# One decoder layer on one core: the input normalised in three token groups ahead of the memory tokens

## The reference

```python
n1 = rms_norm(x, g_mix)                        # x * rsqrt(mean(x*x) + 1e-6) * g_mix
qa, ka, va, qr, kr, vr, gr = split(n1 @ w_in)  # 512, 128, 128, 256, 256, 512, 512 columns
att = window_attention(qa, ka, va, sinks)      # window 128, with ALiBi
ret = retention(qr, kr, vr)
h = x + merge(att, groupnorm(ret) * silu(gr)) @ w_out
mn = rms_norm(mem_prompt, g_mem)               # 256 memory tokens
mk, mv = mn @ w_xk, mn @ w_xv                  # needed by the cross attention, and outputs p_mem_k, p_mem_v
h = h + cross_attend(rms_norm(h, g_xattn), mk, mv)
h = h + square(relu(rms_norm(h, g_mlp) @ w_up)) @ w_down
y = rms_norm(h, g_final)
```

## Time and profile before

| what | value |
|---|---|
| median of three runs | 1641.11 us |
| the profiled execution | 1644.39 us, of it the span 1642.6 us |
| PE busy in the span | 1536.9 us (94%) |
| DVE, ACT, POOL busy | 645.1, 442.3, 246.3 us |
| mean granted clock of PE | 0.968 of full speed |

### The profile page before, as it was taken

The page is one execution under the profiler, slowest core; times in us unless marked ns, Lnnn a source line. Parts: engine busy times, 40 slices in busy tenths (PEclk is TensorE's granted clock), DMA queues, the critical chain, the costliest instruction groups (busy, mean ns, idle before and its releaser), DMA issues.

```text
span 1642.6 us, 25177 instructions
## 1 busy us (share of the span) xinstructions
PE 1536.9 (94%) x9990; PEld 1479.1 (90%) x9990; DVE 645.1 (39%) x1169; ACT 442.3 (27%) x791; POOL 246.3 (15%) x276
## 2 busy tenths in 40 slices
PE   5959999989699999788999999999999999999998
PEld 5959988878599999787888999999999999999997
DVE  3542466455644442243337432234322332233322
ACT  3541244333311111242214331123201330123212
POOL 2010000042236600112435000000000000000143
PEclk9979999999779999899999999999999999999999
DMA  5751110020332131022553111111111111111112
GB/s 175 211 207 44 35 39 14 14 62 13 121 114 58 41 101 39 13 103 91 167 167 103 42 48 52 38 52 41 49 51 39 51 39 52 51 40 51 39 39 106
DMA packets 152618, 115.38 MB, mean 70 GB/s; under 512 B 12880, under 2 KB 141968, under 8 KB 152272
## 3 DMA queue, kind: packets, MB, share of 16 engines
q1 hardware_dynamic: 140816, 72.49, 15.3%
q0 software_dynamic: 10576, 37.66, 6.6%
q10 hardware_dynamic: 1152, 4.19, 0.7%
HBM read 101.19 MB, written 14.16 MB: 70 GB/s over the span
## 4 chain that ended last, share of the span: by engine, by line
PE 82%; issue 7%; DVE 5%; DMA 3%; ACT 2%; POOL 1%; SPq 0%; DVEq 0%; ACTq 0%; POOLq 0%
PE ps L351 23%; PE ps L352 23%; PE ps L353 23%; PE ps L1047 4%; PE ps L1333 2%; PE ps L1351 2%; DVE wlo L340 1%; PE ps L1110 1%; PE ps L1131 1%; DMA raw<-in_w_xv 1%; ACT whi L324 1%; DVE xlo L1478 1%; DMA raw<-in_w_xk 1%; PE ps L1197 0%; DMA out_p_mem_v<-mkv 0%
## 5 line engine op out<-in xcount | busy, mean ns | idle before, releaser
L351 PE MATMUL ps<-xhi,whi 128*128 128x352 f32 x1392 | 457.7, 329 | 15.7 <-DVE wlo L340 8.3
L352 PE MATMUL ps<-xlo,whi 128*128 128x352 f32 x1392 | 450.0, 323 | 0.0
L353 PE MATMUL ps<-xhi,wlo 128*128 128x352 f32 x1392 | 449.6, 323 | 0.0
L351 PE MATMUL ps<-yhi,whi 128*128 128x352 f32 x1152 | 374.1, 325 | 5.9 <-DVE wlo L340 2.1
L352 PE MATMUL ps<-ylo,whi 128*128 128x352 f32 x1152 | 370.1, 321 | 0.0
L353 PE MATMUL ps<-yhi,wlo 128*128 128x352 f32 x1152 | 369.9, 321 | 0.0
L351 PEld LDWEIGHTS ps<-xhi,whi 128*128 128x128 f32 x1392 | 264.9, 190 | 23.6 <-issue 12.5
L352 PEld LDWEIGHTS ps<-xlo,whi 128*128 128x128 f32 x1392 | 265.0, 190 | 0.1
L353 PEld LDWEIGHTS ps<-xhi,wlo 128*128 128x128 f32 x1392 | 264.1, 190 | 0.0
L324 ACT ACTIVATE whi<-raw 128x1024 fp32r<-128x1024 f32 x126 | 132.9, 1055 | 427.9 <-PE ps L353 400.9
L351 PEld LDWEIGHTS ps<-yhi,whi 128*128 128x128 f32 x1152 | 216.9, 188 | 8.6 <-DVE wlo L340 3.9
(11 more groups left out here) (267 smaller groups left out, 1353.1 us busy)
## 6 DMA issues: line engine op xcount, KB each, us to landing
raw<-in_w_up SPq DMA_DIRECT2D x32, 512.0 KB
raw<-in_w_down SPq DMA_DIRECT2D x32, 512.0 KB
raw<-in_w_xo SPq DMA_DIRECT2D x16, 512.0 KB
kx<-in_cache_mem_k POOLq DMA_DIRECT2D x16, 512.0 KB, 5.0
raw<-in_w_in SPq DMA_DIRECT2D x14, 512.0 KB, 3.8
spill<-hT POOLq DMA_DIRECT2D x8, 528.0 KB, 6.2
hT<-spill POOLq DMA_DIRECT2D x8, 528.0 KB, 5.1
raw<-in_w_xk SPq DMA_DIRECT2D x8, 512.0 KB
```

What stands on the lines that cost most here:

```text
L351: pe.matmul(out, whi[:, q, k, :], x1, start=k == 0, stop=False)
L352: pe.matmul(out, whi[:, q, k, :], x2, start=False, stop=False)
L353: mm = pe.matmul(out, wlo[:, q, k, :], x1, start=False, stop=k == KB - 1)
```

## The change

The order of the first stages is turned round, and the x tokens are taken in three groups of 384, 384 and 288.

- **Loads.** SP issues them: identity and ones first, then the x tiles into nine buffers, with the first two units set between them, and all later units in one order. ACT issues the load of `g_mix`. POOL loads memory tokens, the rest of the tables and the other vectors later.
- **Groups.** As soon as three tiles are turned and copied, ACT and DVE make `xhi` and `xlo` of this group alone, and only then the squares, 1/rms and diagonals. 1/rms is a power -0.5 on POOL (`mean_root`); the root and reciprocal on ACT and DVE go away.
- **First two units** (keys, values): chunk by chunk over both units, as each group comes (`first_product`).
- **Memory units.** Order of units: keys, values, query unit 0, eight units of `w_xk`, query unit 1, eight units of `w_xv`, query units 2 and 3. The memory tokens are turned inside query unit 0, the memory keys turned back inside query unit 1, the memory values inside query unit 2 (16 transposes each), each stored when its copies are done.
- **Places.** `xin`, `diag`, `mnhi` and `mnlo` lie behind `za`'s sixth block, `mkvT` and `mkv` over `hT`; so DVE waits for the residual spill ahead of the memory units and for the stores of the memory keys and values ahead of unit `U_RET`, where `zb` takes the place.

The core of the diff (line numbers of the new kernel differ):

```diff
+FIRST = ["k", "v", 0] + ["mk"] * 8 + [1] + ["mv"] * 8 + [2, 3]
+CHUNKS = [1 if f in ("mk", "mv") else NCH for f in FIRST]
+U_Q0, U_MK, U_Q1, U_MV = 2, 3, 11, 12
+U_IN = 16
...
@@ SP
+            sp.dma_start(tab[:, 0:2 * P], io["tables"][:, 0:2 * P]).then_inc(s_first, 16)
+            for t in range(3):
+                x_load(t)
+            first_unit(0)
+            x_load(3)
+            first_unit(1)
+            for t in range(4, XT):
+                x_load(t)
+            for u in range(2, U_RET):
+                first_unit(u)
@@ POOL
+            pool.wait_ge(S("dve_constants"), 3)
+            mean_root(0, 0, 3)
+            pool.wait_ge(*x_ready(5))
+            pool.dma_start(memx[:], io["mem_prompt"][0].rearrange("(t p) d -> p t d", p=P)).then_inc(s_tab, 16)
+            pool.dma_start(tab[:, 2 * P:], io["tables"][:, 2 * P:]).then_inc(s_tab, 16)
...
             for k in range(KB):
                 pool.dma_start(spill[k], hT[:, k, :]).then_inc(s_spill, 16)
+            mean_root(2, 6, XT)
+            mean_root(3, XT, XT + 2)
@@ ACT
+                act.dma_start(gains[:, G_MIX, :], io["g_mix"][0].rearrange("(k p) -> p k", p=P)).then_inc(s_first, 16)
...
+            act.wait_ge(s_first, 32)
...
+            for t in range(3):
+                x_keep(t)
+            split_hi(act, 0, 0)
+            first_hi(0)
+            x_keep(3)
+            squares_x(0)
+            split_hi(act, 1, 1)
+            x_keep(4)
+            x_keep(5)
+            rstd_x(0)
+            first_hi(1)
+            squares_x(1)
...
+            for u in range(U_MK, U_IN + 4):
+                split_hi(act, u + 1, (u + 1) % 2)
+                if u == U_Q1:
+                    kv_keep(0)
+                    kv_keep(2)
@@ PE
+            for t in range(4):
+                turn_x(t)
+            first_product(0, 0)
+            turn_x(4)
+            turn_x(5)
+            spread_rstd(0)
+            first_product(1, 0)
+            turn_x(6)
+            first_product(0, 1)
+            turn_x(7)
+            turn_x(8)
+            spread_rstd(1)
+            first_product(1, 1)
+            first_product(0, 2)
+            spread_rstd(2)
+            first_product(1, 2)
...
+            for u in range(U_MK, U_Q1):
+                pe.wait_ge(s_wlo, u + 1)
+                product(pe, u, u % 2, 0, mnhi, mnlo, NM)
+            u = U_Q1
+            pe.wait_ge(s_wlo, u + 1)
+            product(pe, u, 1, 0, xhi, xlo, CW)
+            pe.wait_ge(s_ev, chunks_before(u))
+            for s in range(4):
+                turn_kv(s)
...
@@ DVE
+            def first_evacuate(q, c):
+
+                dve.wait_ge(s_rstd, c + 1)
+                dve.wait_ge(s_mm, 2 * c + q + 1)
+                dve.tensor_tensor(za[:, 4 + q, c * CW:(c + 1) * CW], ps[:, q, 0:CW], rstd[:, c * CW:(c + 1) * CW], ALU.mult).then_inc(s_ev, 1)
...
-            dve.wait_ge(s_mout, 48)
-            run(U_IN, 2, scaled(za, U_IN - 4))
-            run(U_IN + 2, 2, scaled(za, U_IN + 2))
...
+            dve.wait_ge(s_spill, 16 * KB)
+            for u in range(U_MK, U_IN + 4):
+                split_lo(dve, u + 1, (u + 1) % 2)
...
-            dve.wait_ge(s_spill, 16 * KB)
+            dve.wait_ge(s_mout, 48)
             for n in range(NQ):
```

More of the change, by code:

```diff
@@ L120, in tables, with chunks_before @@
     return t.astype(np.float32), s.astype(np.float32)
-def chunks_before(u, memory=False):
-    if memory or (isinstance(u, int) and u <= U_IN):
-        return u
+def chunks_before(u):
+    if isinstance(u, int) and u < U_RET:
+        return sum(CHUNKS[:max(u, 0)])
     return u * 3 - 2 * U_IN
@@ new lines, in x_keep, with first_hi @@
+            def x_keep(t):
+                w = P if t < NQ else TS
+                act.wait_ge(s_xT, t + 1)
+                copy(hT[:, 0:4, t * P:t * P + w], ps[:, 2 + 2 * (t % 2), :].rearrange("p (k t) -> p k t", k=4)[:, :, 0:w]).then_inc(s_xea, 1)
+            def first_hi(g):
+                for k in range(KB):
+                    act.wait_ge(s_xea if k < 4 else s_xed, min(3 * g + 3, XT))
+                    act.activation(xhi[:, k, group(g)], hT[:, k, group(g)], ACT.Copy, scale=gains[:, G_MIX, k:k + 1]).then_inc(s_fhi, 1)
@@ new lines, in square, with squares_x, rstd_x @@
+            def square(n, w, in_):
+                wait(act, s_sqx, n)
+                act.activation(ss[0:w, 0:D], in_, ACT.Square, accum_out=sqx[0:w, n:n + 1]).then_inc(s_sqx, 1)
+            def squares_x(g):
+                for t in range(3 * g, 3 * g + 3):
+                    w = P if t < NQ else TS
+                    square(t, w, xin[0:w, t, :])
+            def rstd_x(g):
+                act.wait_ge(s_nmm, g + 1)
+                w = group(g).stop - group(g).start
+                copy(rstd[:, group(g)], ps[:, 6 + g % 2, 0:w]).then_inc(s_rstd, 1)
@@ new lines, in _ @@
+            act.wait_ge(s_first, 32)
+            act.wait_ge(S("dve_constants"), 3)
+            for t in range(3):
[10 more added lines that the diff above has]
+            squares_x(1)
+            for t in range(6, XT):
+                x_keep(t)
+            rstd_x(1)
+            first_hi(2)
@@ L748, in square_x @@
[L748 to L779, removed]
+                act.activation(mnhi[:, k, :], ps[:, 2 + k // 2, (k % 2) * NM:(k % 2) * NM + NM], ACT.Copy, scale=gains[:, G_MEM, k:k + 1]).then_inc(s_fhi, 1)
+            def kv_keep(s):
+                act.wait_ge(s_mt, s // 2 * 2 + 1)
+                copy(mkv[:, s // 2 % 2, s // 4 * D:s // 4 * D + 512], ps[:, 2 + s % 4, :]).then_inc(s_mta, 1)
@@ L1085, in _ @@
-            pe.wait_ge(s_xea, XT)
-            pe.wait_ge(s_xed, XT)
-            for s in range(8):
-                if s >= 4:
-                    pe.wait_ge(s_mta if s % 2 == 0 else s_mtd, (s - 4) // 2 + 1)
-                for j in range(4):
-                    mm = turn(ps[:, 2 + s % 4, j * P:(j + 1) * P], mkvT[:, (s % 4) * 4 + j, (s // 4) * P:(s // 4 + 1) * P])
-                mm.then_inc(s_mt, 1)
-            pe.wait_ge(s_rstd, 3)
-            pe.wait_ge(s_lo, KB - 1)
-            units(U_IN, 4, xhi, xlo, last_block=(s_lo, KB))
@@ L1100, in win_turn_v @@
+            for s in range(4):
+                turn_kv(s)
+            product(pe, u, 1, 1, xhi, xlo, CW)
+            product(pe, u, 1, 2, xhi, xlo, CW)
+            for u in range(U_MV, U_IN + 4):
+                pe.wait_ge(s_wlo, u + 1)
+                product(pe, u, u % 2, 0, mnhi, mnlo, NM)
             def win_turn_v(n):
@@ L1138, in _ @@
             pe.wait_ge(s_ev, chunks_before(u))
+            pe.wait_ge(s_mta, 2)
+            pe.wait_ge(s_mtd, 2)
+            for s in range(4, 8):
+                turn_kv(s)
             win_turn_v(0)
+            pe.wait_ge(s_mta, 3)
+            pe.wait_ge(s_mtd, 3)
             win_scores(0, 0)
@@ L1441, in _ @@
                 if f == 0:
-                    units(u0, 8, xhi, xlo, last_block=(s_lo, 4 * KB), before=lambda c: norm_sum(3) if c == 1 else None)
+                    units(u0, 8, xhi, xlo, last_block=(s_lo, 3 * KB), before=lambda c: norm_sum(3) if c == 1 else None)
                 else:
@@ new lines, in first_lo, with mean_squares @@
+            def first_lo(g):
+                for k in range(KB):
+                    if k < 4:
+                        dve.wait_ge(s_xea, min(3 * g + 3, XT))
+                    else:
+                        dve.wait_ge(s_xed, min(3 * g + 3, XT))
+                    dve.wait_ge(s_fhi, KB * g + k + 1)
+                    dve.scalar_tensor_tensor(xlo[:, k, group(g)], hT[:, k, group(g)], gains[:, G_MIX, k:k + 1], xhi[:, k, group(g)].bitcast(F32), ALU.mult, ALU.subtract).then_inc(s_flo, 1)
+            def mean_squares(n, a, b):
+                dve.wait_ge(s_sqx, b)
+                dve.tensor_scalar(msx[:, a:b], sqx[:, a:b], 1.0 / D, EPS_N, ALU.mult, ALU.add).then_inc(s_ms, 1)
@@ new lines, in _ @@
+            dve.wait_ge(s_first, 32)
+            for t in range(3):
+                x_keep(t)
+            split_lo(dve, 0, 0)
+            first_lo(0)
+            x_keep(3)
+            mean_squares(0, 0, 3)
+            split_lo(dve, 1, 1)
+            diagonals(0)
+            x_keep(4)
+            x_keep(5)
+            first_evacuate(0, 0)
+            first_lo(1)
+            first_evacuate(1, 0)
+            x_keep(6)
+            mean_squares(1, 3, 6)
+            diagonals(1)
+            x_keep(7)
@@ L1558, in _ @@
[L1558 to L1566 removed]
+                                         ALU.mult, ALU.subtract).then_inc(s_flo, 1)
```

292 lines of the change are left out of this document (158 added, 134 removed).

## The result

| what | before | after |
|---|---|---|
| median of four runs each, side by side | 1642.65 us (1636.73 to 1647.57) | 1617.72 us (1616.75 to 1622.36) |
| the profiled execution, and its span | 1644.39, 1642.6 us | 1617.97, 1616.2 us |
| PE's first product starts | 22.90 us | 17.98 us |
| mean granted clock of PE | 0.968 | 0.973 |

The ratio is 0.9855, with a 95% interval of 0.9817 to 0.9894: 1.5% faster, 24.9 us between the medians and 26.4 between the two spans. The forecast was 1613, with a range of 1604 to 1625.

A forecast was written before the change was run, and what follows sets the result against it. PE is busy for 94% of the span, so time was to be had only ahead of 119 us. 17.9 + 47.5 + 49.9 + 14.2 gave 129.5, like for like 28.3 us earlier: 1613 against the median of 1641.1, range 1604 to 1625.

The forecast's parts named there:

- first product: Start of PE's first product, after three x tiles, weight splits and the first group's `xlo`: 17.9 us, 22.9 before.
- nine chunks, turns and late waits: First product to end of query unit 0: 44.4 us of PE work plus 3.0 of late waits, 47.5, to 65.4.
- sixteen memory units: Units of `w_xk` and `w_xv`: four at PE's 2.87 us, twelve at the load-and-split pace of 3.2; 49.9, to 115.3.
- query unit 1: Three chunks of 3.82 us, 16 transposes 1.75, and 1.0 for its load in two halves: 14.2, to 129.5.
- start of unit `U_IN + 4`: Where the rebuilt front ends: forecast at 129.5 us, 159.9 before.
- gain, like for like: At unit `U_IN + 4`, counting transposes (1.75) and copies (0.3) that now follow inside it: 131.6 against 159.9, 28.3 us earlier.
- the lower end: Load of `g_mix` on ACT's queue ahead of the first product: 3.8 us taken, from a span of 3.8 to 9.5.
- Late loads: Rival at the start: slow `g_mix` makes tiles 5.0 us later, or spaced loads the first product 7.4; 1618 to 1621, chance 0.12.
- The three late places: PE's waits among the nine chunks: group two's `xlo` 0.9, group three's `xlo` 0.8, its diagonals 1.3; together 3.0 us.
- Two fast units in each eight: Memory units: behind each query unit the loads are ahead, so two of eight go at PE's pace, 2.87 us each.
- DVE's wait for the stores: Ahead of `U_RET`: values stored at about 136, landing 8.07 us later at 144, wanted at 154; the wait costs nothing.
- There I expect the two traces to run alike, shifted: Sign for the program after 190 us: nothing there gives the time back; otherwise the forecast is wrong.

The follow-up runs named there:

- The third slot: The changed kernel with a third slot of `raw` for the weights of units ahead of `U_RET`, lying in an x tile's place: 1614.91 us, ratio 0.9802.
- the run with squares first: The changed kernel with ACT taking the three squares of each group before its high part (`xhi`): 1628.58 us, ratio 0.9892.

## Why the prediction was right, step by step

| step | forecast | measured |
|---|---|---|
| first product | 17.9 | 17.98 |
| nine chunks, turns and late waits, to 65.4 | 47.5 | 47.1, to 65.09 |
| sixteen memory units | 49.9 | 49.7 (24.84 and 24.85) |
| query unit 1 | 14.2 | 13.4 |
| start of unit `U_IN + 4` | 129.5 | 128.15 |
| gain, like for like | 28.3 | 29.5 |
| what is lost behind it | 0 | 3.1 in this trace |

- **The first product** came as reckoned, and the lower end was right for `g_mix`. The Trainium skill's rule in *DMA: Bandwidth & Descriptors*, Rules for kernel authors, held in the count: the queue that took the load went from 1152 packets to 2192, 1040 more. It did not decide the time: 1024 descriptors of 4 bytes landed in 2.3 us, beside loads of 512 KB. *Late loads* is out as to `g_mix`. One wait was left out of the sum: PE turns the fourth tile ahead of the first product, and for that tile it stood until 15.90. It cost next to nothing, because `xlo` ended only at 17.8: luck, as far as the sum goes.
- **The nine chunks** were right in sum by errors that cancel. The first chunk took 5.1 us and not 6.3, since the clock rose 2.7 us after its start and not 5.5. The three late places cost 0.87, 0.81 and 0.48, for 0.9, 0.8 and 1.3; the third was priced too high. Against that the eight other chunks took 3.81 to 3.97 each instead of 3.82, together 0.7 more, and the turns and the spreading some 0.8 more than priced.
- **The memory units** went at the price of a load that no x tiles slow down (3.78 and 3.88 in the chain). The third slot shows that it is this cycle that sets their pace. Two fast units in each eight came as forecast: the first two took 2.87 or 2.88 each, the other six 3.18 in the mean. With all units in a row only the first two are fast, as the reason given for it asks, but the other fourteen take 3.13 in the mean and all sixteen 49.5: the two units' gain is lost again in the others.
- **Query unit 1** has no 1.0 us for a load in two halves; its one wait, 0.34, stands in the memory units.
- **DVE's wait for the stores** costs nothing: the store of the values was issued at 135.34 and took 4.4 us, not 8.07, well ahead of 154. The run with this wait alone moved shows what it is worth, some 5.4 us, more where the first chunk runs at 2.4 GHz.
- **"There I expect the two traces to run alike, shifted"** failed. They run alike in what is done, not in the clock: 1.4 us go between 290 and 930, 1.7 in the closing stores. So the spans are 26.4 apart and not 28.3, although the front gained 1.2 more than forecast. The medians are only 24.9 apart, since the profiled execution of the kernel before lies 1.7 above its median of four and that of the change 0.3. The forecast of 1613 was off by 4.7 us: the price of the front is borne out, the claim that nothing is lost behind it is not, and 1.5 of the 4.7 come from a median before of 1642.65 instead of 1641.11.

Shown by single runs are the groups (14.7 us), the store's wait (5.4 to 6.8) and that the slot still holds back 3.1 to 3.8. If the parts add, some 8 to 9 of the 29.5 us are left, for the earlier start, the cheaper turning of memory tokens and the shorter loads; they are read from the trace and were not tried alone.

## What to carry to other kernels

Where a whole normalisation stands between two product stages, cut the tokens in groups, and let the engines that split and scale work one group ahead of the products; put what the product itself needs (the high and low part) ahead of what only its evacuation needs (squares, 1/rms). Price such a change from the steady pace of like instructions and the chain of waits, and check it at a landmark that both kernels have: behind it, executions of one kernel can differ by more than what you look for. A wait of 4 us on PE's path costs more than itself, since the clock falls behind it: 1.4 us more in the run with squares first, 2.4 in the kernel before.

## What the runs showed of the hardware

- The clock does not fall at the same moment after equal waits. In the run with squares first both waits were 4.27 us. Behind the first the matmuls were slow at once (0.63, then 0.49 us each, from 37.91 to 40.98). Behind the second five ran at the full rate before it fell, and it was low from 54.82 to 58.27.
- Nor does it rise at the same moment. The kernel before and the run with the store's wait moved do the same up to the first input unit, 0.55 us apart. In the one the clock rose with the second matmul (107.21), in the other with the thirteenth (109.85).
- The first products after the start were slow for 2.7 us in the change and for about 5.5 us before.
- A load of 4 KB in 1024 pieces lands in 2.3 to 2.9 us from ACT's queue, in the change and in four of its variants; on POOL's queue, behind larger loads, it took 9.5.
